# Two transformer blocks in split fp32: inner activations rounded first and split on VectorE, identity products during the norms, and block 2's parameters turned later

## What is computed

```python
def first_block(x, c, ...):                      # DEPTH = 2, D_FF = 2816
    for l in range(DEPTH):
        mod = (silu(c) @ ada_w[l] + ada_b[l])
        sh1, sc1, g1, sh2, sc2, g2 = jnp.split(mod, 6, axis=-1)
        h = rmsnorm(x, norm_mix_g[l]) * (1.0 + sc1) + sh1
        x = x + g1 * (mixers(h @ w_in[l]) @ w_out[l])
        h = rmsnorm(x, norm_ffn_g[l]) * (1.0 + sc2) + sh2
        f = (jax.nn.silu(h @ ffn_w1[l]) * (h @ ffn_w3[l])) @ ffn_w2[l]
        x = x + g2 * f
    return rmsnorm(x, final_g)

def second_block(x, p, ...):                     # DEPTH = 2
    for i in range(DEPTH):
        h = x @ w_in[i]
        mix = mixers_2(h) @ w_o[i]
        x = layer_norm(ALPHA * x + mix, ln1_g[i], ln1_b[i])
        gate, up = jnp.split(x @ w_ffn_in[i], 2, axis=-1)
        ffn = (jax.nn.silu(gate) * up) @ w_ffn_out[i]
        ple = (p[i] @ w_ple[i]) * jax.nn.sigmoid(x @ w_ple_gate[i])
        x = layer_norm(ALPHA * x + ffn + ple, ln2_g[i], ln2_b[i])
    return x
```

## Time and profile before

| | |
|---|---|
| median of three runs | 2603.14 us (2600.03 to 2608.05) |
| the profiled execution, its time | 2609.34 us |
| its span in the trace | 2607.6 us |
| mean granted clock of TensorE | 0.969 |
| TensorE busy | 2455.7 us (94%), 13182 products |
| VectorE busy | 1592.9 us (61%) |
| ScalarE busy | 1047.3 us (40%) |
| GpSimd busy | 1059.3 us (41%) |

### The profile page before, as it was taken

How to read it: one execution, slowest core, us unless ns; L and a number is a source line. 1 busy time by engine, 2 the same in 40 slices (tenths; PEclk the granted TensorE clock), 3 DMA queues, 4 the chain that set the end, 5 groups by cost and what they waited for, 6 DMA issues and landing times.

```text
span 2607.6 us, 33465 instructions
## 1 busy us (share of the span) xinstructions
PE 2455.7 (94%) x13182; PEld 2043.2 (78%) x13182; DVE 1592.9 (61%) x2388; ACT 1047.3 (40%) x1713; POOL 1059.3 (41%) x615
## 2 busy tenths in 40 slices
PE   7799899999999999999999989999989998999997
PEld 4576788987676788988797768898869776888885
DVE  5798686963478674634477466453467747645445
ACT  4225442333425543433433554333444355433342
POOL 0233353534233255345145345534514534553441
PEclk8899999999999999999999999999999999999998
DMA  7513355552321433233232113323322111333330
GB/s 276 179 49 113 97 164 162 182 172 83 98 89 53 146 125 104 92 103 97 83 82 73 49 65 97 105 90 100 110 79 76 63 55 63 106 102 97 97 114 32
DMA packets 243348, 268.76 MB, mean 103 GB/s; under 512 B 19592, under 2 KB 211832, under 8 KB 242936
## 3 DMA queue, kind: packets, MB, share of 16 engines
q1 hardware_dynamic: 243192, 266.63, 31.7%
HBM read 264.51 MB, written 2.10 MB: 102 GB/s over the span
## 4 chain that ended last, share of the span: by engine, by line
PE 73%; DVE 13%; issue 4%; DMA 3%; ACT 3%; POOL 2%; SPq 1%; DVEq 0%; ACTq 0%; POOLq 0%
PE bank L2711 23%; PE bank L2713 22%; PE bank L2712 22%; DVE m_cv L2156 2%; DVE r L1825 2%; DVE k_lo L1972 1%; DMA raw<-in_ffn_w 1%; POOL w_lo L1570 1%; PE bank L3302 1%; ACT k_hi L1036 1%; DMA b_raw<-in_ada_w 1%; POOL k_lo L1581 1%; ACT w_hi L982 1%; DVE g_acc L1825 1%; PE bank L3335 1%
## 5 line engine op out<-in xcount | busy, mean ns | idle before, releaser
L1581 POOL TENSOR_TENSOR k_lo<-raw,k_hi 128x512 fp32r<-128x512 f32 x288 | 394.8, 1381 | 712.5 <-ACT k_hi L1036 709.6
L1036 ACT ACTIVATE k_hi<-raw 128x512 fp32r<-128x512 f32 x528 | 324.3, 627 | 510.7 <-PE bank L2713 413.1
L1570 POOL TENSOR_TENSOR w_lo<-raw,w_hi 128x2048 fp32r<-128x2048 f32 x53 | 253.2, 4777 | 563.1 <-ACT w_hi L982 481.1
L2711 PE MATMUL bank<-h_hi,k_lo 128*128 128x512 f32 (+1 forms) x1240 | 432.1, 348 | 13.8 <-DVE h_lo L1932 10.9
L2712 PE MATMUL bank<-h_lo,k_hi 128*128 128x512 f32 (+1 forms) x1240 | 430.8, 347 | 0.0
L2713 PE MATMUL bank<-h_hi,k_hi 128*128 128x512 f32 (+1 forms) x1240 | 430.3, 347 | 0.0
L2711 PE MATMUL bank<-h_hi,w_lo 128*128 128x512 f32 (+1 forms) x784 | 323.4, 413 | 38.6 <-DVE h_lo L1932 13.7
L2712 PE MATMUL bank<-h_lo,w_hi 128*128 128x512 f32 (+1 forms) x784 | 312.8, 399 | 0.0
L2713 PE MATMUL bank<-h_hi,w_hi 128*128 128x512 f32 (+1 forms) x784 | 312.1, 398 | 0.0
L2711 PE MATMUL bank<-f_hi,k_lo 128*128 128x512 f32 x704 | 281.3, 400 | 23.1 <-POOL f_lo L1601 15.3
L2712 PE MATMUL bank<-f_lo,k_hi 128*128 128x512 f32 x704 | 277.7, 394 | 0.0
(11 more groups left out here) (388 smaller groups left out, 4653.2 us busy)
## 6 DMA issues: line engine op xcount, KB each, us to landing
raw<-in_ffn_w SPq DMA_DIRECT2D x60, 1024.0 KB, 5.3
raw<-in_w_ffn_in SPq DMA_DIRECT2D x44, 1024.0 KB, 5.1
raw<-in_w_in SPq DMA_DIRECT2D x34, 1024.0 KB
b_raw<-in_ada_w SPq DMA_DIRECT2D x32, 1024.0 KB, 5.2
raw<-in_w_ffn_out SPq DMA_DIRECT2D x16, 1024.0 KB, 5.1
z_a<-in_ada_w SPq DMA_DIRECT2D x4, 2048.0 KB, 14.0
g_raw<-in_ada_w SPq DMA_DIRECT2D x8, 1024.0 KB, 5.2
raw<-in_w_out SPq DMA_DIRECT2D x8, 1024.0 KB
```

The source lines that it names most:

```text
L1036: act.activation(hi, src, ACT.Copy).then_inc(s.f_hi.up, 1)
L1570: pool.tensor_tensor(b.w_lo[p][:, 0:n], b.raw[p][:, 0:n], b.w_hi[p][:, 0:n].bitcast(F32), ALU.subtract)\
L1581: pool.tensor_tensor(lo, src, hi.bitcast(F32), ALU.subtract).then_inc(s.f_lo.up, 1)
L2711: pe.matmul(out, wlo, xhi, start=start, stop=False)
```

## The change

- **A.** Where the unit after a gate pair is `down` (three places in each of the four feed-forwards), ScalarE rounds `f_hi` at part 0, directly behind silu, ahead of the `k_hi` refills of that step, and the subtraction `f_lo` moves from GpSimd to VectorE, directly behind `gated`. The other gate pairs keep their order.
- **B.** `keep_busy` makes 19 products of the identity by itself, 128x512, into a bank that the next products overwrite: in `first_units` of both layers of block 1, ahead of any wait, and in `pe_first_pair` in block 1's second layer and in all four of block 2 (mixer and feed-forward of both layers), behind the waits for `w_lo` and the banks. Seven places.
- **C.** `first_units` waits for two slots in each of its four steps, where it waited for all eight first, and frees one slot after each of the first three steps and the other five at the end.
- **D.** The norm loops do `h_lo` of tile 0 behind the second root, where it came behind the third.
- **E.** `parameters()` comes behind the first pair in block 2's second layer too.

```diff
+BUSY = 19
@@ act_ffn
-        if part == 1 and old is not None:
+        if old is not None and part == (0 if kind == "down" else 1):
             hidden(old)
         for q in plan.after[t]:
             act_high(act, e, lay, q)
@@ pool_ffn
-        if part == 1 and plan.gate_done(u) is not None:
+        if part == 1 and plan.gate_done(u) is not None and plan.units[u][0] != "down":
             hidden(plan.gate_done(u))
@@ dve_rms (the same edit in dve_layer_norm and dve_shift_norm)
-        if k > 1:
+        if k == 1:
+            dve_low(dve, e, c, 0, full, low, half)
+        if k > 2:
             dve_low(dve, e, c, k - 2, full, low, half)
@@ dve_ffn
+    def hidden_low(i):
+        for m in range(2):
+            at = i % SPARE * 2 + m
+            dve.wait_ge(*s.fh(n, 2 * i + m + 1))
+            dve.tensor_tensor(b.f_lo[:, at, :], b.f_full[:, m, :], b.f_hi[:, at, :].bitcast(F32), ALU.subtract)\
+               .then_inc(s.fl.up, 1)
...
             gated(plan.gate_done(u))
+            if kind == "down":
+                hidden_low(plan.gate_done(u))
@@
+def keep_busy(pe, e, out):
+    eye = e.b.eye_r[:, :].unsqueeze(1).to_broadcast([P, NB, P])
+    for _ in range(BUSY):
+        pe.matmul(out[:, :].rearrange("p (a c) -> p a c", a=NB), e.b.eye_r[:, :], eye, start=True, stop=True)
@@ pe_first_pair
+    if busy:
+        keep_busy(pe, e, outs[0][0])
     for k in range(KD):
         pe.wait_ge(*ready(k))
@@ first_units
-        for q in range(RING):
-            pe.wait_ge(*s.low_in(n, plan, q))
+        keep_busy(pe, e, bank[0])
         for k in range(4):
+            for q in (k, 4 + k):
+                pe.wait_ge(*s.low_in(n, plan, q))
...
-        op.then_inc(s.f_step.up, RING)
+            op.then_inc(s.f_step.up, 1 if k < 3 else RING - 3)
@@ block 1, first pair of the mixers
-                  between=later if l == 0 else None)
+                  between=later if l == 0 else None, busy=l > 0)
@@ block 2
-    if l:
-        parameters()
     pe_first_pair(...)
-    if l == 0:
-        parameters()
+    parameters()
```

More of the change, by code:

```diff
@@ L2355, in dve_layer_norm @@
             dve_normed(dve, e, l * 2, 0)
-        if k > 1:
+        if k == 1:
+            dve_normed_low(dve, e, l * 2, 0)
+        if k > 2:
             dve_normed_low(dve, e, l * 2, k - 2)
@@ L2467, in dve_shift_norm @@
             centre(k + 2)
-        if low and k > 1:
+        if low and k == 1:
+            dve_normed_low(dve, e, l * 2 + 1, 0)
+        if low and k > 2:
             dve_normed_low(dve, e, l * 2 + 1, k - 2)
@@ L2746, in pe_unit_at, with pe_first_pair @@
             between()
-def pe_first_pair(pe, e, u, ready, outs, rows=P, between=None):
+def keep_busy(pe, e, out):
+    eye = e.b.eye_r[:, :].unsqueeze(1).to_broadcast([P, NB, P])
+    for _ in range(BUSY):
+        pe.matmul(out[:, :].rearrange("p (a c) -> p a c", a=NB), e.b.eye_r[:, :], eye, start=True, stop=True)
+def pe_first_pair(pe, e, u, ready, outs, rows=P, between=None, busy=True):
     s, b = e.s, e.b
```

## The result

The changed kernel takes 2574.55 us at the median of four runs (2568.72 to 2577.70), beside 2601.59 for the kernel before (2599.09 to 2608.05): a ratio of 0.9890, 95% interval 0.9864 to 0.9916. That is 27 us less by the medians and 28.6 by the ratio. A second set of six runs on another occasion gave 0.9894 (0.9874 to 0.9914), with a median of 2571.58. The forecast was 2565, within a range of 2553 to 2584.

The account below looks back on a forecast made before the run. TensorE, holding 73% of the chain of waits, bounds the kernel through idle time and low clock. A 20.9, B, D, E 14.5 and C 2.9 make 38.3; 2609.34 less that is 2571.0, less 6.2 gives 2565 us, range 2553 to 2584.

Parts of the forecast that it names:

- Part A, 20.9 us: TensorE's four waits for f_lo: 14.7 of 15.3 us go, and 6.2 us of half clock behind them; from 10.4 to 21.5.
- The remaining 0.6 us: f_lo waits expected to stay: 0.3 us at each of two block 1 places, where GpSimd's k_lo run beside VectorE.
- Less 6.2 for the median: Forecast moved down from 2571.0 because the median of three runs, 2603.14, was 6.2 below the profiled execution, 2609.34.
- B's main term: Seven stretches behind the norms, 35.44 us at half clock, would run at full clock: 16.6 us saved.
- Two places behind a w_lo, -1.2 and -2.3: Block 1's second layer, block 2's start: later start, -1.2; identity products partly at half clock, also at block 2's second layer, -2.3.
- Block 1's feed-forwards: Gains behind the norms there from faster clock, earlier h_lo (0.6 us each) and part C's earlier slot release (2.9 us).
- 2.9 of part C: First refill in block 1's feed-forwards: both k_lo waits, 1.45 us each, go because slots come free some 6 us earlier.
- Parts D and E: Earlier h_lo saves 0.6 twice, 0.3 twice and 0.95 us; the parameters' transposes cost 1.3: +1.4 us.
- (1): Rival: identity products run at half clock for about 5 us, only the rest fast; B gives 3.8, time 2576; chance 0.20.
- (3): Rival: f_lo's wait is replaced by later k_hi at all 12 places, 13.6 us lost, time 2579; chance 0.08.
- (2): Rival: identity products neither hold nor raise the clock, real products start 23.2 us later in all, time 2602; chance 0.05.
- (4): Rival: identity products on one bank don't overlap, 0.63 us each, 12.0 us per place, time 2629; chance 0.03.

Follow-up runs that it names:

- the order alone: ScalarE's half of part A on the kernel before: f_hi ahead of the k_hi refills, f_lo still on GpSimd; ratio 1.0004 (0.9989 to 1.0018).
- VectorE alone: Other half of part A on the kernel before: f_lo on VectorE, f_hi rounded in its old place behind the k_hi refill; ratio 1.0007 (0.9992 to 1.0022).

## Why the prediction was right, and where it was off

The direction and the range were right, and so was part A, which carried most of it: 21 of some 27 us. The second cause, the norms' clock, was right in its mechanism (1.00 granted at all seven places), but its worth was not: 14.5 us forecast for B, D and E together, and 4 to 5, not clear of the noise, measured for the identity products. The gain was put at 38 us where 27 to 29 were measured. The steps one by one:

- **Part A, 20.9 us, measured 21 by the ratio and 19.5 by the medians.** The remaining 0.6 us in two block 1 places came out as 0.32 each. But 0.69 us for f_lo was not the value where it counted: at the ends of all four feed-forwards the second f_lo took 1.77 us or more, in block 1 the first one too, and the slack of 2 us covered it. That the sum held is in part luck. Nor did all 24 take the slow value: eight took 0.85 to 1.80 us, sixteen 0.69. In the profiles the four places are worth 6.8, 6.3, 2.6 and 5.8 us, 21.5 in all.
- **Less 6.2 for the median.** The execution of before that the sum was made from was a long one: 2609.34 us, where 29 later runs have a median of 2598.15. The sum counted part of that excess as a gain, and then 6.2 us of it were taken off the time once more: without that the forecast would have been 2571.0, beside 2574.55 and 2571.58 measured. The 33.6 us between the profiles are near the sum of 38.3, in part by luck, since 4.5 of them come from two places in block 1's first layer whose code no part edits. One is 2.2 us ahead of the first feed-forward, where the wait for mf was 5.4 us and then 3.0; in the traces of the other kernels it is now the one and now the other. The other is 2.3 us around 547, where the trace of before has a stretch at half clock (548.2 to 551.6) and that of the changed kernel none. The medians are 27 apart. And one term was taken from that execution as if it were fixed, the half-clock stretches behind the norms:

```profile
1275.99:1278.99 3.00, 3.00 (x7) 0.50 0.57 160
```

```profile
1275.59:1281.74 6.15, 6.15 (x15) 0.50 0.80 216
...
sum 30.15, PE 30.14; mean PE 4.31
```

```profile
1278.78:1281.93 3.15, 3.15 (x8) 0.50 0.65 170
...
sum 32.30, PE 32.30; mean PE 4.61
```

These are windows of three kernels in which that code is as before (part C alone, the order alone, VectorE alone): the first line is each time the stretch at the start of block 2, the sum that over the same seven places. It is 6.16 us in the earlier trace rows, and 3.00, 6.15 and 3.15 here. The seven together are 35.44, 30.15 and 32.30. For the same instructions the clock comes back after 3 us or after 6. B's main term, 0.47 x 35.44 = 16.6, was read off the longest of them; with 30.15 it is 14.2.
- **Two places behind a w_lo, -1.2 and -2.3.** In the profile they cost 2.1 and 2.4 us of start, 4.5 against 3.5 reckoned (the 2.3 also held the third place); in another execution 0.5 and 2.4. The mechanism was right. What I missed is that the identity products could stand ahead of the wait for w_lo.
- **Block 1's feed-forwards, some 8 us of the sum** (2.7 + 1.5 of clock, 0.6 twice, 2.9 of part C). This is the step that failed: "on a chain of ScalarE and VectorE that starts with that release; it now starts some 6 us earlier". It starts earlier, onto GpSimd's u_t_lo, and VectorE loses 5 us on three k_lo. Between the profiles TensorE gains 3.6 and 2.5 us by the end of `first_units` and its next units, and within the first unit of the last matrix it has lost all of it (-0.6 and 0.1 left, where 8 had been reckoned). That the kernel without C is no slower agrees with a pace set by VectorE.
- **Parts D and E.** Block 2's other places gained 3.0, 1.6 and 3.0 us between the profiles, about what B, D and E had been given there. The order of the norm alone was not tried, but the kernel with `BUSY = 0` has it without identity products: its gap behind the norm's sums is 0.6 us shorter than before at the six places other than block 2's second layer (4.87 for 5.47 at the first), so 0.3 was too little for block 2. The eight transposes of the parameters took 1.10 us at 1929.02, as the earlier trace rows said, and the kernel with B alone showed that E had to come with B, by 4.3 us.
- **The rivals.** (1) and (3) came near in time (2576 and 2579, where 2574.55 and 2571.58 were measured), and (1) is nearer than the forecast, but their mechanisms are out. For (1): the identity products hold the clock where they follow at once, and where they start cold, it is back before they end. For (3): waits for k_lo at all twelve places, 13.6 us, did not come; all of them together are 2.6 us. (2) and (4) are out, at 2602 and 2629, and by the traces: the clock is 1.00 through and behind the nineteen, and they start 0.23 us apart.

What stays open: whether the 38 identity products of block 1's feed-forwards are worth anything, how much of the 4 to 5 us for all of them is real, where part C alone gets its 3.9 us, the norm's order in a run of its own, and what decides after how long the clock returns in one execution and another.

## What to carry to other kernels

When a result has to come through two queues and each of them alone is late enough to hold it, take it out of both or leave it: here each move alone was worth nothing. Ask of every wait that is removed which engine sets the end of the stretch, and follow an earlier start to what GpSimd runs beside it. And read the price of a clock that falls and comes back from several executions, not from the one profile at hand.

## What the runs showed of the hardware

- A VectorE subtraction of 128x512 with two inputs takes 0.69 us alone and 0.85 to 1.80 beside a GpSimd subtraction. The 24 f_lo of the changed kernel have 693 ns at the median and 1798 at most, and the two at the end of block 1's first feed-forward took 3.50 us together.
- Products of the identity that write one bank again and again, each opening and closing its sum, start 0.23 us apart when the clock is full (nineteen in 4.59 to 4.92 us), as products of a long sum do.
- Nineteen of them held the clock over a wait of 4.2 to 4.9 us at four places in each of two executions of the changed kernel, with gaps of up to 0.6 us behind them. Behind a gap of 2.72 us it had fallen. After an idle time of 1.24 us ahead of them the clock was down in one execution and up in another, with the same code.
